# Last head's pages gathered in its first half, first output tile's rows split during the sample attention, loops over groups and tiles written out

## The reference

```python
h = rms_norm(x, norm_pre);  z = h @ w_in            # 1024 wide in, columns split among three branches and a gate
# A: latent attention: q = rms_norm(c_q) @ w_uq, keys and values from the 128-wide latent c_kv and a rotary key
#    prompt: causal over 2048 tokens; samples: over 2048 cached positions, fetched by page_table, and the 4 new ones
o_att = attend(...)                                 # 8 heads x 64
# B: trailing means over 2/4/8/16 tokens, minus the token, through pool_w and pool_scale
# C: GLU -> causal depthwise convolution of width 31 -> LayerNorm -> silu -> conv_pw
mixed = concat([o_att, y_pool, y_conv]) * silu(gate)
y = x + rms_norm(mixed @ w_out, norm_post)
```

## Time and profile before

| | |
|---|---|
| median of 3 runs | 1438.33 us (1436.21 to 1442.11) |
| profiled execution | 1440.17 us, of which the span is 1438.5 us |
| TensorE busy | 1302.1 us (91%), 7300 matmuls |
| VectorE, ScalarE, GpSimd busy | 837.4, 634.5 and 491.5 us |
| stage 1 / 2 / 3 / 4 | about 0 to 457 / 457 to 945 / 945 to 1012 / 1012 to 1438.5 us |
| mean granted TensorE clock | 0.951 of full speed |

### The profile page before, as it was taken

How to read it: one execution, slowest core, us unless ns; L and a number is a source line. 1 busy time by engine, 2 the same in 40 slices (tenths; PEclk the granted TensorE clock), 3 DMA queues, 4 the chain that set the end, 5 groups by cost and what they waited for, 6 DMA issues and landing times. The chain is left out here.

```text
span 1438.5 us, 22291 instructions
## 1 busy us (share of the span) xinstructions
PE 1302.1 (91%) x7300; PEld 1064.2 (74%) x7300; DVE 837.4 (58%) x1802; ACT 634.5 (44%) x1278; POOL 491.5 (34%) x424
## 2 busy tenths in 40 slices
PE   4889989889865999999999999978699999999996
PEld 3768768677534788888888888855578888888883
DVE  3468676676764988888888888733233232414231
ACT  5424242341422777777777777723322121212210
POOL 4236145351462244415234330059222231313121
PEclk9999989999875999999999999979899999999998
DMA  7534161341526033122232222572551323223110
GB/s 239 147 106 142 39 223 47 103 158 38 194 35 119 20 88 98 46 80 62 72 88 49 66 70 63 156 222 61 182 155 59 117 77 98 94 81 113 48 51 18
DMA packets 140616, 141.17 MB, mean 98 GB/s; under 512 B 54901, under 2 KB 109782, under 8 KB 139062
## 3 DMA queue, kind: packets, MB, share of 16 engines
q1 hardware_dynamic: 132294, 111.99, 26.8%
q0 software_dynamic: 5360, 17.68, 4.3%
q10 hardware_dynamic: 2880, 10.49, 2.2%
HBM read 103.89 MB, written 46.71 MB: 105 GB/s over the span
## 5 line engine op out<-in xcount | busy, mean ns | idle before, releaser
L1289 ACT ACTIVATE pT<-tp 128x512 fp32r<-128x512 f32 (+2 forms) x320 | 168.6, 532 | 106.6 <-PE tp L1228 97.0
L1346 DVE TENSOR_SCALAR_CACHE_REDUCE prob<-sc 128x512 f32<-128x512 f32 (+2 forms) x320 | 192.9, 603 | 31.7 <-PE sc L1220 17.6
L1355 DVE TENSOR_TENSOR big<-tp,pT 128x512 fp32r<-128x512 f32 (+2 forms) x320 | 193.8, 607 | 26.5 <-ACT pT L1289 26.0
L1977 PE MATMUL m<-w_gate,big 128*128 128x512 f32 x816 | 196.0, 399 | 10.1 <-POOL big L1942 10.1
L1977 PEld LDWEIGHTS m<-w_gate,big 128*128 128x128 f32 x816 | 152.8, 189 | 46.5 <-POOL big L1942 10.3
L2098 DVE SCALAR_TENSOR_TENSOR shared<-m,rq,g_post 128x512 f32<-128x512 f32 (+1 forms) x34 | 23.9, 745 | 262.5 <-POOL rq L1954 262.5
L1228 PE MATMUL tp<-ident,prob 128*128 128x128 f32 x1088 | 171.9, 273 | 0.9 <-DVE big L1355 0.9
L1279 ACT ACTIVATE prob<-prob,nm 128x1024 f32<-128x1024 f32 (+2 forms) x192 | 171.7, 894 | 1.6 <-DVE nm L1349 1.2
L701 DVE SCALAR_TENSOR_TENSOR acc<-aT,cols,acc 128x512 f32<-128x512 f32 x232 | 163.2, 751 | 13.0 <-DVE qst L777 6.4
L1228 PEld LDWEIGHTS tp<-ident,prob 128*128 128x128 f32 x1088 | 128.6, 141 | 25.2 <-issue 1.7
L894 PE MATMUL mm<-big,w_in 128*128 128x512 f32 x576 | 141.7, 404 | 5.6 <-ACTq L585 5.6
(11 more groups left out here) (273 smaller groups left out, 2334.5 us busy)
## 6 DMA issues: line engine op xcount, KB each, us to landing
xtok<-in_x ACTq DMA_DIRECT2D x20, 512.0 KB, 4.3
xraw<-in_xT SPq DMA_DIRECT2D x17, 512.0 KB, 3.9
QT<-qst SPq DMA_DIRECT2D x32, 256.0 KB, 3.2
LAT<-in_cache_ckv SPq DMA_DIRECT2D x128, 64.0 KB, 2.1
big<-Y SPq DMA_DIRECT2D x16, 512.0 KB, 5.1
shared<-in_x SPq DMA_DIRECT2D x16, 512.0 KB, 4.0
out_y<-shared SPq DMA_DIRECT2D x16, 512.0 KB, 2.8
raw<-QT SPq DMA_DIRECT2D x7, 1024.0 KB, 5.2
```

What stands on the lines that cost most here:

```text
L1289: act.activation(pT[0][:, 4 * c:4 * c + w // P, (t % 4) * P:(t % 4 + 1) * P], tp[n % NTP][:, 0:w].rearrange("p (k q) -> p k q", q=P), ACT. ...
L1346: dve.tensor_scalar(prob[:, slot[m % J], 0:w], sc[b][:, 0:w], -1.0, None, ALU.mult, ALU.min, accum_out=top).then_inc(sc_free[b], 1)
L1355: dve.tensor_tensor(cut(1), tp[n % NTP][:, 0:w].rearrange("p (k q) -> p k q", q=P), f32(cut(0)), ALU.subtract)\
L1977: last = pe.matmul(out, w(pw_, k), x(px, k), start=(k == 0 and q == 0), stop=(k == n - 1 and q == 2))
```

## The change

Four edits. (1) The loops over groups (stage 1) and over tiles (stage 4) become plain Python loops, so each trip is written out on every engine, with constant semaphore values. (2) In the last head, the sixteen pages are gathered as eight before the store of column group 0 and eight before that of group 1, none before groups 2 and 3. (3) The first tile's rows of x are loaded by SP in stage 3 into a buffer of their own, ACT rounds them after the first half's value products, and DVE subtracts; stage 4 skips the load, the copy and POOL's split of tile 0. (4) So that the split can be kept, the tile buffers `hT`, `m2` and `yt` move to `q2a` and `k2a`, and four chunks of `w_out` move from there to `big`.

```diff
@@ over_groups
-            with eng.Fori(1, GROUPS) as it:
+            for it in range(1, GROUPS):
                 group(Group(it, False), Group(it - 1, False))
@@ stage2, sync engine
                     for g in range(4):
                         pieces(g)
-                        gather(h, range(g * N_PAGES // 4, (g + 1) * N_PAGES // 4))
+                        parts = 4 if h < HEADS - 1 else 2
+                        if g < parts:
+                            gather(h, range(g * N_PAGES // parts, (g + 1) * N_PAGES // parts))
                         sp.wait_ge(s["ost"], i * 8 + hf * 4 + g + 1)
@@ stage3
+        xraw0, hT0 = keep["xraw0"], tile_hT(keep)[:, 0, :, :, :]
...
+                sp.dma_start(xraw0[:, :, :], a["xT"][:, 0:P].rearrange("(k p) n -> p k n", p=P)).then_inc(s["x0"], 16)
                 for i in range(2):
                     sp.wait_ge(s["oatt"], i + 1)
...
                 copies(1, 3)
+                act.wait_ge(s["pv"], 1)
+                act.wait_ge(s["x0"], 16)
+                act.activation(hT0[:, 0, :, :], xraw0[:, :, :], ACT.Copy).then_inc(s["x0_hi"], 1)
                 exps(1)
...
                 heads_out(0)
+                dve.wait_ge(s["x0_hi"], 1)
+                dve.tensor_tensor(hT0[:, 1, :, :], xraw0[:, :, :], f32(hT0[:, 0, :, :]), ALU.subtract).then_inc(s["x0_lo"], 1)
                 top(1, 3)
...
+def tile_hT(keep):
+    return keep["q2a"][:, :, :].rearrange("p i n -> p (i n)").rearrange("p (b i k n) -> p b i k n", b=2, i=2, k=KC)
@@ stage4
-        held = [t[:, :, k * D_MODEL:(k + 1) * D_MODEL] for t in (keep["q2a"], keep["k2a"]) for k in range(2)]
+        big = keep["big"][:, :, :].rearrange("p k n -> p (k n)").rearrange("p (i k n) -> p i k n", i=2, k=4)
+        held = [big[:, :, k, :] for k in range(4)]
...
-        hT = big[:, 0:4 * D_MODEL].rearrange("p (b i k n) -> p b i k n", b=2, i=2, k=KC)
-        m2 = big[:, 4 * D_MODEL:6 * D_MODEL].rearrange("p (i k n) -> p i k n", i=2, k=MC)
-        yt = f32(big[:, 6 * D_MODEL:]).rearrange("p (b k n) -> p b k n", b=2, k=MC)
-        xraw = sb("xraw", [P, 2, KC, P])
+        hT = tile_hT(keep)
+        m2 = keep["k2a"][:, 0, :].rearrange("p (i k n) -> p i k n", i=2, k=MC)
+        yt = f32(keep["k2a"][:, 1, :]).rearrange("p (b k n) -> p b k n", b=2, k=MC)
+        xraw = (keep["xraw0"], sb("xraw1", [P, KC, P]))
...
-            with eng.Fori(0, NT // 2) as i:
+            for i in range(NT // 2):
                 for hf in range(2):
                     f(Tile(i, hf))
...
-                load_x(0, 0, False)
+                sp.sem_inc(x_ld[0], 16)
                 load_x(1, 1, False)
...
-                split(0, 0)
+                pool.sem_inc(s["split"], 1)
+                pool.sem_inc(s["xT_free"], 1)
                 split(1, 1)
-                with pool.Fori(0, NT // 2 - 1) as i:
+                for i in range(NT // 2 - 1):
...
                     act.activation(rs[:, b:b + 1], rstd_all[:, bass.ds(T2, 1)], ACT.Copy).then_inc(s["cols"], 1)
+                    if T2 == 0:
+                        act.sem_inc(s["x_hi"], 1)
+                        return
```

More of the change, by code:

```diff
@@ L1496, in stage3 @@
         s = {n: sem(n) for n in ("prep", "q", "rot", "tdone", "sdone", "new", "snew", "mx", "nm", "exp", "den", "pv", "olat", "att", "oatt",
-                                 "out", "zero", "w", "g_pre", "kr")}
+                                 "out", "zero", "w", "g_pre", "kr", "x0", "x0_hi", "x0_lo")}
         w_ld = [sem(f"w_ld{i}") for i in range(2)]
@@ L1851, in stage4 @@
         stage = sb("stage4", [P, WB, D_MODEL])
-        big = keep["big"][:, :, :].rearrange("p k n -> p (k n)")
-        hT = big[:, 0:4 * D_MODEL].rearrange("p (b i k n) -> p b i k n", b=2, i=2, k=KC)
-        m2 = big[:, 4 * D_MODEL:6 * D_MODEL].rearrange("p (i k n) -> p i k n", i=2, k=MC)
-        yt = f32(big[:, 6 * D_MODEL:]).rearrange("p (b k n) -> p b k n", b=2, k=MC)
-        xraw = sb("xraw", [P, 2, KC, P])
+        hT = tile_hT(keep)
+        m2 = keep["k2a"][:, 0, :].rearrange("p (i k n) -> p i k n", i=2, k=MC)
+        yt = f32(keep["k2a"][:, 1, :]).rearrange("p (b k n) -> p b k n", b=2, k=MC)
+        xraw = (keep["xraw0"], sb("xraw1", [P, KC, P]))
         gate = sb("gate", [P, D_MIX])
@@ L1890, in load_x @@
                         sp.wait_ge(s["xT_free"], t - 1)
-                    sp.dma_start(xraw[:, b, :, :], a["xT"][:, bass.ds(t * P, P)].rearrange("(k p) n -> p k n", p=P)).then_inc(x_ld[b], 16)
+                    sp.dma_start(xraw[b][:, :, :], a["xT"][:, bass.ds(t * P, P)].rearrange("(k p) n -> p k n", p=P)).then_inc(x_ld[b], 16)
                 def store(t, n, b):
@@ L1916, in _ @@
                 tile(Tile(0, 1), back=False)
-                with sp.Fori(1, NT // 2 - 1) as i:
+                for i in range(1, NT // 2 - 1):
                     for hf in range(2):
@@ L1941, in split @@
                     pool.wait_ge(s["x_hi"], t + 1)
-                    pool.tensor_tensor(hT[:, b, 1, :, :], xraw[:, b, :, :], f32(hT[:, b, 0, :, :]), ALU.subtract).then_inc(s["split"], 1)
+                    pool.tensor_tensor(hT[:, b, 1, :, :], xraw[b][:, :, :], f32(hT[:, b, 0, :, :]), ALU.subtract).then_inc(s["split"], 1)
                     pool.wait_ge(s["split"], t + 1)
@@ L2007, in _ @@
                 gates(0, 0)
-                with pe.Fori(0, NT // 2) as i:
+                for i in range(NT // 2):
                     for hf in range(2):
@@ L2029, in x_hi @@
                     act.activation(rs[:, b:b + 1], rstd_all[:, bass.ds(T2, 1)], ACT.Copy).then_inc(s["cols"], 1)
+                    if T2 == 0:
+                        act.sem_inc(s["x_hi"], 1)
+                        return
                     act.wait_ge(x_ld[b], i * 16 + 16)
-                    act.activation(hT[:, b, 0, :, :], xraw[:, b, :, :], ACT.Copy).then_inc(s["x_hi"], 1)
+                    act.activation(hT[:, b, 0, :, :], xraw[b][:, :, :], ACT.Copy).then_inc(s["x_hi"], 1)
                     act.wait_ge(s["x_hi"], T2 + 1)
@@ L2059, in tile @@
                     squares(T)
-                with act.Fori(0, NT // 2 - 1) as i:
+                for i in range(NT // 2 - 1):
                     for hf in range(2):
@@ L2129, in build @@
                 stage2(nc, a, keep)
-                with nc.sbuf_tensor("w_gate", [P, 2, KC, D_MIX], F32R) as w_gate:
-                    keep["w_gate"] = w_gate
+                with nc.sbuf_tensor("w_gate", [P, 2, KC, D_MIX], F32R) as w_gate, nc.sbuf_tensor("xraw0", [P, KC, P], F32) as xraw0:
+                    keep |= {"w_gate": w_gate, "xraw0": xraw0}
                     stage3(nc, a, keep)
```

## The result

The kernel after takes 1424.33 us (median of 4 runs, 1422.58 to 1426.71), before 1437.32 in the same measurement: ratio 0.9904, interval 0.9877 to 0.9932. Timed again later beside the experiments it had 1423.44 and the ratio 0.9904 (0.9881 to 0.9926). That is 13 to 14 us faster; the forecast was 1434.1 with a range from 1427, so the change was worth about three times what I gave it. The profiled execution took 1422.58 us, its span is 1420.8, and the mean clock 0.956.

The account below looks back on a forecast made before the run. TensorE was taken to bound stage 4, w_out transfers its start, store waits stage 1, SP stage 2's end. 1440.17 - 0.2 - 3.5 + 2.0 - 2.5 = 1436.0 us, at the median 1434.1; range 1427 to 1442.5.

Parts of the forecast that it names:

- The buffers' new places cost nothing: Stage 4: moved buffers add no time, as the same engines read and write the same shapes; no term in the sum.
- My last paragraph: Signs to check; stage 4 tiles differing from 23.27 us would mean straight code costs fetching or buffer places matter.
- Stage 4's loops: Stage 4: writing out the tile loops saves 0.2 us in all, for branches and leaving the loop.
- Stage 1's loops: Stage 1: writing out the groups' loop saves 3.5 us, bounds 0 and 6.
- Rival (a): Stage 1's loops cost all that group 0 lacks, 5.7 us, and the clock is regained: 1430.0 us; chance 0.24.
- the tile loop's 0.02 us: Stage 4: the loop's back branch costs TensorE 0.02 us a trip, read as disagreeing with the skill's branch rule.
- Pages: Last head of stage 2: stores behind eight pages issue the last store 2.0 us later; bounds -0.5 and +4.5.
- side branch: Last head: if TensorE resumes at half clock after its stop, up to 1.8 us more, the write 2.8 later.
- Rival (c): Last head: the store behind eight pages decides, +4.5 there, nothing from the loops: 1442.1 us, slower; chance 0.12.
- First tile's rows: Stage 4's start: splitting the first tile in stage 3 saves 2.5 us, 1.6 from earlier chunks; bounds 0.5 and 4.
- The 0.9 for the clock: Stage 4's first tile: half of the 1.76 us lost after TensorE's stop is regained; bounds 0 and 2.

Follow-up runs that it names:

- e3_place: The kernel before with only buffers moved: hT, m2 and yt into q2a and k2a, four w_out chunks into big; 1434.50 us, ratio 0.9950.
- e2_loops4: The kernel after with stage 4's five loops put back, all else kept; 1427.57 us, ratio 0.9905 to before.
- e9_late: The kernel after with the first tile's rows loaded and split in stage 4 again; 1426.10 us, ratio 0.9906 to before.
- e11_diff256: The kernel before with hT, m2, yt and w_out chunks moved as in after, big at a multiple of 512, k2a 256 past one; 1428.03 us, one run.

## Why the prediction was wrong

**The step that failed** is "The buffers' new places cost nothing: the same shapes are read and written on the same engines." I held duration to follow from shape and engine. The runs show 6.6 ns a matmul by where its two operands lie. e3_place gives the placement alone 6 us, 0.9950, and the tile goes from 23.28 to 22.87 us in after, e3_place and e2_loops4 alike. In before `big` lay at 17120, 224 past a multiple of 512, and its partners `w_gate`, `q2a`, `k2a`, `v2a` and `w_out_b` at 256: a distance of 32 in all 96 matmuls of a tile. In after, `hT` and `m2` are in `q2a` and `k2a`, so 72 of 96 have distance 0 and the 24 with a chunk in `big` still 32. With this term the forecast would have been 1428. My last paragraph named it ("that the new places of the buffers matter"), but I gave it neither a term nor a chance, and so it widened no bound.

The Trainium skill (SBUF — State Buffer, Operand start alignment) asks only that an operand start at a multiple of its element size, 4 bytes for fp32. All starts here do, and the times still differ; no trace here contradicts the page, which speaks of what is allowed and not of speed.

**Stage 4's loops**, 0.2: right; e2_loops4 shows the time of after and 22.87 us a tile.

**Stage 1's loops**, 3.5 with bounds 0 and 6: measured 3.6, by 16 traces. That it came so near is partly luck: 3.5 was a choice between two bounds. Rival (a)'s 5.7 is too much. (Its sum also takes 1.6 for the pages, where the forecast has 2.0, without saying why.)

The Trainium skill's rule on taken branches (Runtime: NRT & Kernel Launch, Instruction fetch mechanics) has the right sign here. It speaks of a stall only where the branch's target lies outside the pages of code that the engine holds. The prediction left that condition out, so the tile loop's 0.02 us does not contradict the page, and no run here shows which case either loop is.

That the excess is a fetch at the branch is not shown. In before it lies in the waits of DVE for stores and of PE behind them, and which of them the loop lengthens stays open.

**Pages**, 2.0: measured 2.3 by PE and 3.0 by SP's issues, inside its bounds. The first half of the mechanism is as forecast, DVE's wait for the store behind eight pages. The second is not. The 2.0 let DVE's last write wait for the second store; in after it waits 2.98 us for ACT, as it did in before. To the stop is added that TensorE runs at half clock behind it: in all five traces with two parts the last write comes 17.7 to 18.3 us behind the write before it, and 15.5 or 15.6 in the ten with four. The prediction had priced this as a side branch, 2.8 later, and did not take it. That the 2.0 came near is in part luck. Rival (c) needed 4.5 there and no gain elsewhere, and falls.

**First tile's rows**, 2.5 with bounds 0.5 and 4: mis-sized. The term is 3 to 3.7 us up to the first transpose, where I had 1.6 for it. Between the two chains the first chunk's transfer starts 1.04 us instead of 2.02 after the stage's first issue and takes 6.05 instead of 7.49 us. I had let issue and transfer overlap; they add, to 2.4.

The 0.9 for the clock stood for the first tile's length, which fell by 2.3 us, 0.4 of it by the placement. Its mechanism is as forecast. In before TensorE stops for 2.97 us ahead of the output product and then takes 12.97 us for it, with the clock granted at 0.5 for 3.4 us. In after the half clock falls on the transposes and the gate product (1.97 us, and 23.99 us for the 96 matmuls, 6 us of it at 0.5), and no stop is left. e9_late stops for 2.70 us, but the clock stays at 1.0 behind it and the product takes 11.31 us.

The size depends on which clock an execution happened to get. In the seven kernels with before's loops and late split the first tile takes 26.3 and 26.5 us with no time at 0.5, 27.4 and 28.1 with 3.4 us of it, and 29.2 to 29.3 with 6.8; in the others it takes 25.8 to 26.9. So 2.3 us is what two traces differ by, and not a fixed price.

**Together**: -3.6 + 2.3 - 3.7 - 2.3 - 6.0 = -13.3 us, against 13.0 between the medians. The terms are read from different sets of traces (for the split e9_late alone would give 3.0 and not 3.7), and the interval of the ratio is about 4 us to either side, so the sum is confirmed no finer than that.

## What to carry to other kernels

When an edit moves operands of TensorE to other buffers, write down the start of each modulo 256 and compare it with its partner's, row pitches included; count the matmuls whose distance changes. Where TensorE bounds a stage, a buffer order that keeps all partners at the same place modulo 256 cost nothing here and was worth 0.6 us a tile (23.28 to 22.66). And when one queue does bookkeeping beside its stores in the stage's last step, try to take the bookkeeping out rather than to rearrange it: rearranging cost 2.3 us, taking it out gave 8.5.

## What was not expected of the hardware

- fp32r matmuls of 512 columns, each with its own load of weights, step at 226.7 ns where the two operands, the weights and what is streamed past them, start at a distance of 0 or 256 bytes modulo 512, and at 233.3, 233.3 and 232.6 ns at 32, 64 and 128. Why was not examined.
- The fast step comes back only after some five matmuls: behind matmuls at a distance of 32 the first two of `w_out_b` with `k2a` still read 232.5 and 230.9 ns in after. Behind the transposes the first few are as uneven, even where all 96 have a fast distance (231.3, 233.5, 227.7, 229.4 and 228.9 ns in e11_diff256). So single rows in a mixed sequence show little.
- After the 8.12 us stop in the last head TensorE's granted clock was 0.50 from 920 to 925 us, and 1.00 in before, where it had stopped for 1.41. The rest of that head took 2.25 us more.
- A loop over stage 1's groups costs 1.2 us a trip over straight code, one over stage 4's tiles nothing that a tile's length shows (22.87 us with and without).
